# First attention of a two-block kernel: scores contract 64 rows in pairs, each half of the keys on its own row half of the array

## What is computed

```
h = rms_norm(x, norm1_g);  z = h @ w_in
q, k, v, xr, yr = split(z)              # q: 8 heads of 64; k, v: 2 heads of 64 (4 q heads share one)
q = axial_rope(rms_norm(q, q_norm_g)) * 64 ** -0.5
k = axial_rope(rms_norm(k, k_norm_g))
s = einsum("qd,sd->qs", q, k)           # per head: 1024 x 1024 scores, contraction over 64 channels
p = softmax(s, axis=-1);  o = p @ v     # no mask
```

## Time and profile before

| | |
|---|---|
| runs | 4095.82, 4097.86, 4097.99 us; median 4097.86 |
| profiled execution, first to last instruction | 4093.9 us (the only time that the profile has of it) |
| mean granted TensorE clock | 0.956 |
| PE busy | 3694.8 us (90%), 17348 matmuls |
| DVE, ACT, POOL busy | 1736.2, 1336.7, 678.1 us |
| the four attentions | from 144 to 471 us, 64 S, 64 T, 32 PV |

### The profile page before, as it was taken

How to read it: one execution, slowest core, us unless ns; L and a number is a source line. 1 busy time by engine, 2 the same in 40 slices (tenths; PEclk the granted TensorE clock), 3 DMA queues, 4 the chain that set the end, 5 groups by cost and what they waited for, 6 DMA issues and landing times.

```text
span 4093.9 us, 44381 instructions
## 1 busy us (share of the span) xinstructions
PE 3694.8 (90%) x17348; PEld 2966.7 (72%) x17348; DVE 1736.2 (42%) x1692; ACT 1336.7 (33%) x1509; POOL 678.1 (17%) x284
## 2 busy tenths in 40 slices
PE   4888836799999995999999999999989979999997
PEld 3776735688888884777788777777766768888885
DVE  5535465432231346222245777777724431111114
ACT  4545462331331224222222333333324132122112
POOL 1000012122222221111111111111111112222221
PEclk8999968999999998999999999999999989999998
DMA  2000002111111110211111101011010211111111
GB/s 90 21 6 16 16 15 77 36 46 46 51 46 46 51 46 21 83 36 36 36 36 42 33 35 36 31 36 36 24 74 26 87 36 46 46 51 47 46 50 68
DMA packets 43130, 174.90 MB, mean 43 GB/s; under 512 B 4784, under 2 KB 4784, under 8 KB 41904
## 3 DMA queue, kind: packets, MB, share of 16 engines
q1 hardware_dynamic: 43056, 173.84, 12.7%
HBM read 161.24 MB, written 12.58 MB: 42 GB/s over the span
## 4 chain that ended last, share of the span: by engine, by line
PE 77%; DVE 13%; issue 4%; ACT 4%; DMA 1%; POOL 0%; DVEq 0%; ACTq 0%; SPq 0%
PE ps L325 62%; PE ps L334 3%; PE ps L1483 3%; DVE conv_acc L1060 3%; PE ps L341 2%; PE ps L1367 2%; PE ps L1360 1%; PE ps L1499 1%; PE ps L1486 1%; DVE h_lo_part L412 1%; PE ps L1493 1%; DVE small L1099 1%; PE ps L1449 1%; DVE lru_e L1247 0%; DVE residual L404 0%
## 5 line engine op out<-in xcount | busy, mean ns | idle before, releaser
L325 PE MATMUL ps<-h_hi_part,w_hi_part 128*128 128x512 f32 x3504 | 1122.9, 402 | 175.4 <-DVE h_lo_part L412 77.7
L305 POOL TENSOR_TENSOR w_lo_part<-w_raw,w_hi_part 128x1024 fp32r<-128x1024 f32 x272 | 661.2, 2431 | 3357.8 <-ACT w_hi_part L298 3357.0
L325 PE MATMUL ps<-h_lo_part,w_hi_part 128*128 128x512 f32 x3504 | 1092.1, 393 | 0.0
L325 PE MATMUL ps<-h_hi_part,w_lo_part 128*128 128x512 f32 x3504 | 1090.1, 392 | 0.0
L325 PEld LDWEIGHTS ps<-h_hi_part,w_hi_part 128*128 128x128 f32 x3504 | 649.6, 191 | 339.0 <-issue 133.4
L298 ACT ACTIVATE w_hi_part<-w_raw 128x1024 fp32r<-128x1024 f32 x272 | 287.7, 1060 | 1616.2 <-PE ps L325 1526.3
L325 PEld LDWEIGHTS ps<-h_lo_part,w_hi_part 128*128 128x128 f32 x3504 | 665.4, 190 | 143.0
L325 PEld LDWEIGHTS ps<-h_hi_part,w_lo_part 128*128 128x128 f32 x3504 | 664.5, 190 | 142.3
L1060 DVE SCALAR_TENSOR_TENSOR conv_acc<-u_pad,cols,conv_acc 128x1024 f32<-128x1024 f32 x232 | 316.5, 1364 | 19.4 <-DVE conv_acc L1060 2.0
L962 DVE TENSOR_TENSOR residual<-residual,ps 128x1024 f32 x56 | 68.3, 1220 | 393.7 <-PE ps L325 393.0
L325 PE MATMUL ps<-u_hi,w_lo_part 128*128 128x512 f32 x736 | 230.9, 394 | 0.0
(11 more groups left out here) (293 smaller groups left out, 3650.9 us busy)
## 6 DMA issues: line engine op xcount, KB each, us to landing
w_raw<-in_w SPq DMA_DIRECT2D x272, 512.0 KB, 3.4
residual<-in_x SPq DMA_DIRECT2D x4, 1024.0 KB, 10.8
residual<-in_x SPq DMA_DIRECT2D x1, 4096.0 KB, 12.4
residual_spill<-residual SPq DMA_DIRECT2D x1, 4096.0 KB, 12.1
conv_spill<-conv_acc SPq DMA_DIRECT2D x8, 512.0 KB, 2.6
conv_again<-conv_spill SPq DMA_DIRECT2D x1, 4096.0 KB, 12.1
residual_again<-residual_spill SPq DMA_DIRECT2D x1, 4096.0 KB, 12.8
out<-residual SPq DMA_DIRECT2D x8, 512.0 KB, 3.0
```

The costliest lines, as they stand in the source:

```text
L305: pool.tensor_tensor(WLO[:, slot], WRAW[:, slot], f32(WHI[:, slot]), ALU.subtract).then_inc(w_ready, 1)
L325: last = pe.matmul(PS[:, slot, b * HALF:(b + 1) * HALF], st[:, slot, k, :], mv[:, k, b * HALF:(b + 1) * HALF], start=(k == 0 and n == 0), ...
```

## The change

q of each head is written to both partition halves of its plane (twice as many ACT and DVE operations in `q_split`), the zeros go, and S(n) is issued as six matmuls with a contraction of 64 rows: keys 0 to 511 on partitions 0 to 63 into the slot's first bank, keys 512 to 1023 on partitions 64 to 127 into its second, in turn.

```diff
-            for t in range(2):
-                other = slice(64, 128) if t == 0 else slice(0, 64)
-                pool.memset(f32(QH[other, t, :]), 0.0).then_inc(zero_ready, 1)
-                pool.memset(f32(QL[other, t, :]), 0.0).then_inc(zero_ready, 1)
-            pool.wait_ge(zero_ready, 4)
...
                 for t in range(2):
-                    act.activation(QH[64 * t:64 * t + 64, t, :], N0[64 * t:64 * t + 64, :], ACT.Copy,
-                                   scale=HD ** -0.5).then_inc(q_hi, 1)
+                    for half in range(2):
+                        act.activation(QH[64 * half:64 * half + 64, t, :], N0[64 * t:64 * t + 64, :], ACT.Copy,
+                                       scale=HD ** -0.5).then_inc(q_hi, 1)
...
-                        nr_act(act, st, jp, u * 2 + 1, lambda: act.wait_ge(q_lo, u * 4 + PRIMED))
+                        nr_act(act, st, jp, u * 2 + 1, lambda: act.wait_ge(q_lo, u * 8 + PRIMED))
...
-                        nr_act(act, st, jp, u * 2 + 2, lambda: act.wait_ge(q_lo, u * 4 + 2 + PRIMED))
+                        nr_act(act, st, jp, u * 2 + 2, lambda: act.wait_ge(q_lo, u * 8 + 4 + PRIMED))
...
                 for t in range(2):
-                    dve.wait_ge(q_hi, a * 2 + (t + 1))
+                    dve.wait_ge(q_hi, a * 4 + (2 * t + 2))
                     rows = slice(64 * t, 64 * t + 64)
-                    dve.scalar_tensor_tensor(QL[rows, t, :], N0[rows, :], HD ** -0.5, f32(QH[rows, t, :]), ALU.mult,
-                                             ALU.subtract).then_inc(q_lo, 1)
+                    for half in range(2):
+                        dve.scalar_tensor_tensor(QL[64 * half:64 * half + 64, t, :], N0[rows, :], HD ** -0.5,
+                                                 f32(QH[rows, t, :]), ALU.mult, ALU.subtract).then_inc(q_lo, 1)
...
-            pe.wait_ge(q_lo, a * 2 + 2 + PRIMED)
+            pe.wait_ge(q_lo, a * 4 + 4 + PRIMED)
...
-                three_pass(pe, 2 + n % 2, QH[:, n % 2, rows], QL[:, n % 2, rows], KH[:, kv, :], KL[:, kv, :]
-                           ).then_inc(s_done, 1)
+                for i, (q, k) in enumerate(((QH, KH), (QH, KL), (QL, KH))):
+                    for b in range(2):
+                        half = slice(64 * b, 64 * b + 64)
+                        keys = slice(HALF * b, HALF * b + HALF)
+                        mm = pe.matmul(PS[:, 2 + n % 2, keys], q[half, n % 2, rows], k[half, kv, keys],
+                                       start=(i == 0), stop=(i == 2))
+                mm.then_inc(s_done, 1)
...
-            pe.wait_ge(zero_ready, 4)
```

More of the change, by code:

```diff
@@ L251, in two_blocks @@
         ss_sum = sem("ss_sum")
-        small_ready, zero_ready = sem("small_ready"), sem("zero_ready")
+        small_ready = sem("small_ready")
         nsq_ready, nsum_done, ny_ready, rope_ready = (sem(n) for n in ("nsq_ready", "nsum_done", "ny_ready", "rope_ready"))
```

## The result

The changed kernel takes 4104.69 us (median of 14 runs, 4101.44 to 4111.89), the kernel before 4095.14 beside it (14 runs, 4092.60 to 4098.34). The ratio is 1.0024, 95% interval [1.0017, 1.0031]: 9.8 us slower, between 7 and 13. That lies just outside "no change" as the prediction drew it (8.2 us) and inside its range; the predicted difference was +5.3. The profiled execution, the fastest of the 14, has a span of 4099.6 us against 4093.9, so the two traces lie only 5.7 us apart; the mean granted clock is 0.956 in both.

A forecast was written before the change was run, and what follows sets the result against it. PE looked like the bound of a steady pair (6.75 us), with ACT's evacuation loop of 6.45 close behind. Terms -7.2 - 4.8 + 14.1 + 3.2 = +5.3 us gave 4103 us from 4097.9; range 4095 to 4128.

The forecast's parts named there:

- steady pairs: Steady part of each attention: PV to PV falls from 6.75 to 6.45, six intervals in each of four attentions, 7.2 us gained.
- four starts: Start of each attention, S(0) to PV(0): shorter scores bring PV(0) 1.2 us sooner, 4.8 us gained over four.
- q into both halves: q_split before each attention: doubled ACT copies and DVE operations cost 3.52 us each time, uncovered, 14.1 us in all.
- clock at the sum: Sum of squares of the next q tile: 4.7 us idle brings half clock, 3.56 against 1.98, 3.2 us for two.
- Scores on half rows, side by side: Score matmuls S: the two row halves overlap, six taking 0.71 plus 0.2 a border in place of 1.41.
- Both rivals about PE's stream: Steady pairs: PE's stream sets the pair, 5.95, 4091 us, chance 0.06; or halves run serially, 7.3, 4128 us, chance 0.12.
- The loop of 6.45: Steady pairs: two transposes, two evacuations and a PV through one slot keep a pair from falling below 6.45 us.
- Borders: Entering and leaving the 64-row form on PE: about 0.40 us for both, taken as 0.2 a border.
- the prediction's signs of being wrong: Changed profile: 6.75 or more between PVs, 5.9 to 6.3, or clock at 0.5 beyond an attention's first 8 us.
- end before the new q_lo, so they add nothing: Splits for a = 0 and 2: ACT's two extra copies and the weight split behind them cost nothing.
- The rival of the clock falling within an attention: Steady pairs: PE's gaps lower the clock; two half-clock pairs per attention add 28 us, 4131; all, over 80; chance 0.07.
- the forecast's likeliest case: Whole kernel: the summed terms give +5.3 us, 4098 to 4110, chance 0.72, about a fifth of it above +8.

The follow-up runs named there:

- the run on one row half: All six 64-row score matmuls put on row half 0, in the kernel with new scores, four PT buffers, weight split and q copies moved: 4113.22 us, ratio 1.0043.
- The four buffers: Four PT buffers for the transposed probabilities in place of two, in the changed kernel: 4084.90 us, ratio 0.9975 against the kernel before.
- Moving the split: ACT's weight split, which releases POOL's L305, moved behind the copy into N0 (L449), in the changed kernel: 4098.36 us, ratio 1.0010 against the kernel before.
- The early sum: ACT's square of the next q tile (L448) no longer waits for q_lo, in the changed kernel: 4097.77 us, ratio 1.0007 against the kernel before.
- the kernel that it is made from: Changed kernel with four PT buffers, square first, weight split and copy into N0 later, q copies for a = 1 and 3 earlier: 4057.64 us, ratio 0.9911.

## Why the prediction was right, and where it was off

The two traces were laid beside each other between points that both have, from the first copy of q to the first convolution of the recurrence: 356.8 us before, 365.6 after, +8.8. The rest of the span differs by -3.1, which is its scatter: over the thirteen traces it spreads by 7 us. Per term:

| term | predicted | measured | where |
|---|---|---|---|
| steady pairs | -7.2 | -7.2 | 24 x (6.75 - 6.45) |
| four starts | -4.8 | -5.8 | S(0) to PV(0) of a = 1: 13.32 to 10.95; of a = 3: -0.76; a = 0 and 2: -1.38, -1.28 |
| q into both halves | +14.1 | +18.2 | 4 x 3.52, and 2 x 2.04 for the remainder beside POOL |
| clock at the sum | +3.2 | +3.7 | 3.78 against 1.98, and what is left over |
| ends | 0 | -0.1 | clock at PV(7) of a = 2 (+1.36), a = 3 (-0.34), and from PV(7) of a = 1 to the next sum (-1.07) |
| sum | +5.3 | +8.8 | |

- **Scores on half rows, side by side: right.** S takes 0.92 for six (predicted 0.71 + 0.2), and the run on one row half shows that nothing but the overlap pays for it. Both rivals about PE's stream fell: the pair is neither 5.95 nor 7.3. In line, S takes 1.59, and the pair 7.11 even with four buffers.
- **The loop of 6.45: right, to the hundredth.** PE waits for ACT's evacuation ahead of both T, as the prediction said. The four buffers show it from the other side: with the loop loosened the pair falls to 6.09. The Trainium skill (TensorEngine Tiling (Array Packing), PSUM Bottleneck) says that the copies out of PSUM may become the bottleneck after a 4x speedup of TensorE; the trace agrees already after one of at most 2x, with 6.45 us for two evacuations, two transposes and a PV.
- **Borders: there.** 0.36 idle of the weight loads going out of the 64-row form and 0.17 going in, 0.53 for both against the estimated 0.40. The Trainium skill (the same page, Key Properties) has TensorE drain at a change of mode; the trace agrees with these two numbers.
- **Four starts: the sum right, the parts not.** Each was to gain 1.2. They gained 2.37 in a = 1, where the clock was full at T(0), as the prediction's other value has it (2.3), 0.76 in a = 3, where half clock lasted 9.3 us from S(0) on (4.6 before), and 1.38 and 1.28. That they add up to 5.8 against 4.8 is in part luck. Half clock beyond an attention's first 8 us was also one of the prediction's signs of being wrong: a = 3 shows it, though the steady pairs ran at full clock.
- **q into both halves: the mechanism right, the size short.** The step that failed is the sentence that ACT's own two extra copies and the weight split behind them "end before the new q_lo, so they add nothing". On ACT that holds. But the split on ACT releases POOL's L305, and the last remainder starts behind it: 3.25 instead of 1.22, at a = 0 and at a = 2. The term measures 18.2, not 14.1. Moving the split brought the four remainders back to 4.97, and the copies alone cost 20.7 us with scores as before, against 17.3 in the prediction's two terms.
- **The clock at the sum: right.** 6.78 idle instead of the predicted 4.7, half clock, 3.78 long. With the weight split moved the idle time was 4.78, and the sum took 3.68. The early sum, after 2.85 idle, took 1.98.
- **The rival of the clock falling within an attention** did not come true: all 24 steady pairs of the changed kernel are 6.45 to 6.46 long.
- **Slower or the same:** with 4 us more for the split the sum is +9.4, and the runs say +9.8 [7, 13]; the forecast's likeliest case had a fifth of its chance there. That the forecast of 4103 lies so near the measured 4104.69 is luck: it starts from a median of three runs, 4097.86, where fourteen give 4095.14, and these 2.7 us hide more than half of what the split was short.

## What to carry to other kernels

A faster step gains no more than the distance to the next loop: read that loop where the step is absent (here the tail of the attention, 6.45 us bare), and look for the wait that closes it. Loosening it, two more buffers, was worth 20 us in the changed kernel, twice what the change itself cost. And when an edit makes a stretch longer on one engine, list what the other engines start meanwhile: the two extra operations of 1.2 us each cost 2.5 and then 2.0 more, because the last of them now came after the start of the engine beside.

## What the runs showed of the hardware

- A VectorE operation with two inputs in SBUF that starts while POOL's weight split runs ends about 1.1 us after the split does (132.41 to 135.66, the split ending at 134.58); one that had begun before the split takes its usual 1.22. In the changed kernel also outside the edit:

```profile
148.85 2.38 POOL L305 TENSOR_TENSOR w_lo_part<-w_raw,w_hi_part 128x1024 fp32r<-128x1024 f32 x1 [14.27 <-ACT w_hi_part L298]
149.06 3.25 DVE L355 SCALAR_TENSOR_TENSOR qk_n<-qk_n,qk_n 128x1024 f32<-128x1024 f32 x1
```

  151.23 is the split's end and 152.31 the operation's, whose own length is 1.23. The Trainium skill (SBUF — State Buffer, Summary: rules for kernel authors) has the second of two such operations wait until the first is done; the trace agrees with 3.25 for 1.23, and with which of the two had begun first.
- The two row halves of TensorE run side by side even when three matmuls of one half stand ahead of those of the other in the code: they started within 0.01 us of each other and S was as short (0.93 against 0.92).
- A 64-row fp32r matmul of 512 columns takes 0.23 us, as at full height. Leaving the 64-row form costs 0.36 us of idle time of the weight loads, and entering it 0.17.
- With all scores on one row half the granted clock stayed at 0.50 from 223 to 240 us with PE busy throughout by the records (10.00 of 10.00 us in the stretch shown). In the kernel that it is made from, with the halves side by side, it was 1.00 from 206 to 223 us, the same part of a = 1, with PE busy for 14.01 of 17.00 us.
